# A diffusion layer's SwiGLU with seven products a tile: its sums of weights by accumulating DMA in place of VectorE

## What is computed

```
def swiglu(h, wg, wu, wd):
    return (jax.nn.silu(h @ wg) * (h @ wu)) @ wd
...
        xs = xs + gt2 * swiglu(modulate(rmsnorm(xs, g_ffn[l]), sh2, sc2), w_gate[l], w_up[l], w_down[l])
```

## Time and profile before

| | us |
|---|---|
| median of 3 runs | 937.9 (936.69 to 941.97) |
| the profiled execution | 939.53 |
| its span (first to last instruction) | 937.7 |
| TensorE busy | 915.8 (98%) |
| VectorE busy | 637.4 (68%) |
| ScalarE busy | 408.1 (44%) |
| GpSimd busy | 2.8 |
| tiles of seven products | 544.96 to 606.56, 662.88 to 761.44, 817.76 to 891.68 |

### The profile page before, as it was taken

One profiled execution on the slowest core, in us unless ns is written; L12 is line 12 of the kernel. 1 busy time (PEld: TensorE's weight loads), 2 busy tenths in 40 slices (PEclk: granted clock), 3 DMA queues, 4 the chain that ended last, 5 costly groups with the idle time before them and its releaser, 6 DMA issues.

```text
span 937.7 us, 15919 instructions
## 1 busy us (share of the span) xinstructions
PE 915.8 (98%) x6385; PEld 859.1 (92%) x6385; DVE 637.4 (68%) x1153; ACT 408.1 (44%) x809; POOL 2.8 (0%) x8
## 2 busy tenths in 40 slices
PE   5999999999999999999999999999999999999998
PEld 4689888778888899999999999999999999999998
DVE  3557898899688752332447989744699954499852
ACT  4663344666777622222246745321344421244430
POOL 0000000000000000000000000000000000000000
PEclk8899999999999999999999999999999999999999
DMA  9844343542445122422202122330222243022331
GB/s 369 325 180 159 139 151 113 162 137 68 136 147 161 54 68 91 180 68 90 68 23 90 46 91 79 102 112 24 82 79 80 78 134 90 24 72 86 116 108 71
DMA packets 33082, 104.44 MB, mean 111 GB/s; under 512 B 3696, under 2 KB 8944, under 8 KB 31856
## 3 DMA queue, kind: packets, MB, share of 16 engines
q1 hardware_dynamic: 32288, 102.64, 33.0%
q10 hardware_dynamic: 720, 0.77, 0.2%
HBM read 99.07 MB, written 4.33 MB: 110 GB/s over the span
## 4 chain that ended last, share of the span: by engine, by line
PE 91%; DVE 4%; DMA 2%; ACT 2%; SPq 1%; issue 1%; ACTq 0%; DVEq 0%
PE ps L1595 38%; PE ps L1952 25%; PE ps L1691 13%; PE ps L1899 4%; PE ps L1817 3%; PE ps L1791 2%; PE ps L1802 2%; PE ps L1644 1%; DMA x<-x_t 1%; PE ps L1715 1%; DMA x<-w_ada 1%; SPq L550 1%; DVE scr L1080 1%; ACT b L626 1%; DVE scr L1231 0%
## 5 line engine op out<-in xcount | busy, mean ns | idle before, releaser
L1043 DVE TENSOR_TENSOR w_lo<-stage,w_hi 128x1024 fp32r<-128x1024 f32 x56 | 68.4, 1222 | 76.5 <-ACT w_hi L613 76.3
L958 ACT ACTIVATE w_hi<-stage 128x512 fp32r<-128x512 f32 x114 | 71.1, 628 | 96.2 <-PE ps L1595 40.7
L1595 PE MATMUL ps<-y_hi,w_hi 128*128 128x320 f32 x480 | 109.4, 309 | 0.0
L1595 PE MATMUL ps<-y_lo,w_hi 128*128 128x320 f32 x480 | 109.3, 309 | 0.0
L1595 PE MATMUL ps<-y_hi,w_lo 128*128 128x320 f32 x480 | 109.3, 309 | 0.0
L613 ACT ACTIVATE w_hi<-stage 128x1024 fp32r<-128x1024 f32 x56 | 59.1, 1061 | 91.7 <-PE ps L1595 50.9
L1952 PE MATMUL ps<-m_hi,w_hi 128*128 128x320 f32 x304 | 93.9, 309 | 0.0
L1952 PE MATMUL ps<-m_lo,w_hi 128*128 128x320 f32 x304 | 93.9, 309 | 0.0
L1952 PE MATMUL ps<-m_hi,w_lo 128*128 128x320 f32 x304 | 93.9, 309 | 0.0
L1595 PEld LDWEIGHTS ps<-y_lo,w_hi 128*128 128x128 f32 x480 | 80.3, 188 | 0.0
L1595 PEld LDWEIGHTS ps<-y_hi,w_hi 128*128 128x128 f32 x480 | 80.2, 188 | 0.0
(11 more groups left out here) (207 smaller groups left out, 1947.6 us busy)
## 6 DMA issues: line engine op xcount, KB each, us to landing
stage<-w_main SPq DMA_DIRECT2D x118, 512.0 KB, 3.6
x<-w_ada SPq DMA_DIRECT2D x23, 512.0 KB, 4.5
qk<-w_ada SPq DMA_DIRECT2D x7, 1024.0 KB, 12.4
bb<-rpb SPq DMA_DIRECT2D x16, 256.0 KB, 4.1
qk<-w_ada SPq DMA_DIRECT2D x5, 512.0 KB, 3.8
x<-x_t SPq DMA_DIRECT2D x1, 2560.0 KB, 10.7
y_t<-x SPq DMA_DIRECT2D x8, 320.0 KB, 2.2
vf<-w_ada SPq DMA_DIRECT2D x4, 512.0 KB, 3.6
```

What stands on the lines that cost most here:

```text
L958: act.activation(w_hi[:, slot, at:at + 512], left_stage(op, g), ACT.Copy).then_inc(left_hi[op], 1)
L1043: dve.tensor_tensor(w_lo[:, slot, :], stage[:, slot, :], w_hi[:, slot, :].bitcast(F32), ALU.subtract).then_inc(lo_done, 1)
L1595: ins = pe.matmul(out[:, half, :], wt[:, w_slot, w], rt[:, rk, half * TH:(half + 1) * TH], start=start and n == 0, stop=stop and n == 2)
```

## The change

GpSimd issues the sums as DMAs that add to their destination (`accum_op=ALU.add`), five transfers of 128 x 512 (256 KB) a tile: S1 adds A22, read again from the weights in DRAM, to A21 in the stage; S3's buffer is loaded with A11 from DRAM, and A21 from DRAM is added; S2 adds S1 to A11, S4 adds S2 to A12, both from SBUF to SBUF. As there is only addition, the signs are turned: the factors are now S2 = A11 + S1, S3 = A11 + A21 and S4 = A12 + S2, and the sums of products subtract the products of S2, S3 and S4. Where one VectorE instruction made two sums at once with one operation, two instructions stand for C11/U2 and for C21/C12. The waits on the sums count by 16, the semaphore steps of a DMA. S2 is split ahead of S1 in the inner loop.

```diff
@@ block.gpsimd
+            def accumulate(op, u, at, done):
+                pool.dma_start(op, w_main[u, :, at:at + 512], accum_op=ALU.add).then_inc(done, 16)
+            for g in range(sum(FF_PARTS) - N_STD):
+                u = gate_unit(N_STD + g)
+                pool.wait_ge(*unit_arrived(u + 1))
+                accumulate(left_stage("S1", g), u + 1, 512, s1_sum)
+                if g:
+                    pool.wait_ge(left_lo["S3"], g)
+                pool.dma_start(s3_sb, w_main[u, :, 0:512]).then_inc(s3_in, 16)
+                pool.wait_ge(s1_sum, 16 * (g + 1))
+                pool.wait_ge(left_lo["A11"], g + 1)
+                pool.dma_start(left_stage("S2", g), left_stage("S1", g), accum_op=ALU.add).then_inc(s2_sum, 16)
+                pool.wait_ge(s3_in, 16 * (g + 1))
+                accumulate(s3_sb, u + 1, 0, s3_sum)
+                pool.wait_ge(s2_sum, 16 * (g + 1))
+                pool.wait_ge(left_lo["A12"], g + 1)
+                pool.dma_start(left_stage("S4", g), left_stage("S2", g), accum_op=ALU.add).then_inc(s4_sum, 16)
@@ block.scalar, left_high
-                    act.wait_ge({"S1": s1_sum, "S2": s2_sum, "S3": s3_sum, "S4": s4_sum}[op], g + 1)
+                    act.wait_ge({"S1": s1_sum, "S2": s2_sum, "S3": s3_sum, "S4": s4_sum}[op], 16 * (g + 1))
...
-                        for op in ("S1", "S2", "S3", "S4"):
+                        for op in ("S2", "S1", "S3", "S4"):
                             left_high(op, g + 1)
@@ block.vector
-            def s3(g):
...
-                dve.tensor_tensor(s3_sb, left_stage("A11", g), left_stage("S1", g), ALU.subtract).then_inc(s3_sum, 1)
-            def s1(g):
...
-                dve.tensor_tensor(left_stage("S1", g), left_stage("S1", g), left_stage("A22", g), ALU.add).then_inc(s1_sum, 1)
-            def s2(g):
...
-                dve.tensor_tensor(left_stage("S2", g), left_stage("S1", g), left_stage("A11", g), ALU.subtract).then_inc(s2_sum, 1)
-            def s4(g):
...
-                dve.tensor_tensor(left_stage("S4", g), left_stage("A12", g), left_stage("S2", g), ALU.subtract).then_inc(s4_sum, 1)
...
-                dve.tensor_tensor(two(H_C11, H_U2), of_product("A12", "S2"),
-                                  by_half[:, H_P1:H_P1 + 1, :].to_broadcast([P, 2, TH]), ALU.add).then_inc(c11_done, 1)
+                dve.tensor_tensor(by_half[:, H_C11, :], of_product("A12"), by_half[:, H_P1, :], ALU.add)
+                dve.tensor_tensor(by_half[:, H_U2, :], of_product("S2"), by_half[:, H_P1, :], ALU.subtract).then_inc(c11_done, 1)
...
-                dve.tensor_tensor(two(H_C21, H_C12), of_product("A22", "S4"), two(H_U3, H_V), ALU.add).then_inc(c12_done, 1)
+                dve.tensor_tensor(by_half[:, H_C21, :], of_product("A22"), by_half[:, H_U3, :], ALU.add)
+                dve.tensor_tensor(by_half[:, H_C12, :], of_product("S4"), by_half[:, H_V, :], ALU.subtract).then_inc(c12_done, 1)
```

More of the change, by code:

```diff
@@ L329, in hybrid_dit_program @@
         s1_sum, s2_sum, s3_sum, s4_sum = (sem(f"s{i}_sum") for i in (1, 2, 3, 4))
+        s3_in = sem("s3_in")
         t_sum, t_hi_done, t_ready = sem("t_sum"), sem("t_hi_done"), sem("t_ready")
@@ L1436, in left_low, with of_product @@
                                   ALU.subtract).then_inc(left_lo[op], 1)
-            def s3(g):
[L1439 to L1442, removed]
-                dve.tensor_tensor(s3_sb, left_stage("A11", g), left_stage("S1", g), ALU.subtract).then_inc(s3_sum, 1)
-            def s1(g):
-                dve.wait_ge(s3_sum, g + 1)
-                dve.tensor_tensor(left_stage("S1", g), left_stage("S1", g), left_stage("A22", g), ALU.add).then_inc(s1_sum, 1)
-            def s2(g):
-                dve.wait_ge(s1_sum, g + 1)
-                dve.tensor_tensor(left_stage("S2", g), left_stage("S1", g), left_stage("A11", g), ALU.subtract).then_inc(s2_sum, 1)
-            def s4(g):
-                dve.wait_ge(s2_sum, g + 1)
-                dve.tensor_tensor(left_stage("S4", g), left_stage("A12", g), left_stage("S2", g), ALU.subtract).then_inc(s4_sum, 1)
-            def of_product(op, op2=None):
-                a, b = BANK_OF[op], BANK_OF[op2 or op]
-                return ps[:, a:b + 1, 0:TH] if op2 else ps[:, a:a + 1, 0:TH].to_broadcast([P, 2, TH])
+            def of_product(op):
+                return ps[:, BANK_OF[op], 0:TH]
             def c11_u2(g):
@@ L1472, in v_sum @@
                 dve.wait_ge(c11_done, g + 1)
-                dve.tensor_tensor(by_half[:, H_V, :], ps[:, BANK_OF["S1"], 0:TH], by_half[:, H_U2, :], ALU.add).then_inc(v_done, 1)
+                dve.tensor_tensor(by_half[:, H_V, :], of_product("S1"), by_half[:, H_U2, :], ALU.add).then_inc(v_done, 1)
             def c22_u3(g):
@@ L1477, in c22_u3 @@
                 dve.wait_ge(v_done, g + 1)
-                dve.tensor_tensor(two(H_C22, H_U3), of_product("S3"), two(H_V, H_U2), ALU.add).then_inc(c22_done, 1)
+                dve.tensor_tensor(two(H_C22, H_U3), two(H_V, H_U2),
+                                  ps[:, BANK_OF["S3"]:BANK_OF["S3"] + 1, 0:TH].to_broadcast([P, 2, TH]),
+                                  ALU.subtract).then_inc(c22_done, 1)
             def c21_c12(g):
@@ L1512, in _ @@
             left_low("A11", 0)
-            s3(0)
             left_low("A12", 0)
-            s1(0)
             gated_up(1)
-            s2(0)
-            s4(0)
             t_low(2)
@@ L1539, in _ @@
                         left_low("A11", g + 1)
-                        s3(g + 1)
                     else:
@@ L1547, in _ @@
                         left_low("A12", g + 1)
-                        s1(g + 1)
                     v_sum(g)
[L1550 to L1553, removed]
+                    if not more:
                         down_low(part, 1)
@@ L1574, in _ @@
                             left_low("A11", g)
-                            s3(g)
                             left_low("A12", g)
-                            s1(g)
-                            s2(g)
-                            s4(g)
                         elif n == 5:
```

## The result

The changed kernel takes 943.49 us in the median of 13 runs (937.9 to 944.83), the kernel before 937.9 us in as many: a ratio of 1.0046 with a 95% interval of 1.0027 to 1.0065. It is slower, by 4.3 us; the forecast had 17.7 us of waiting and a time of 957 us, 19 above the median before. In a second set beside the experiments it took 943.16 us against 938.05, ratio 1.0048 (1.0029 to 1.0068).

A forecast was written before the change was run, and what follows sets the result against it. TensorE was taken to bound the kernel; late sums would make it wait 2.3, 10.4 and 5.0 us in the parts of 5, 8 and 6, together 17.7, so 939.5 + 17.7 = 957 us, range 935 to 1010.

The forecast's parts named there:

- The bound and the cover: FFN tiles: TensorE sets the time without waiting for VectorE, so removing 52 us of VectorE's sums gains 0 us.
- The figure of 49 us: VectorE: its busy time was to be 49 us less in the profile after the change.
- Splitting the instructions: VectorE, twice a tile: two instructions of 320 results for one of 640, 3 us over 19 tiles, hidden under TensorE.
- The loop: S2's sum, S4's sum, then A11's low half releasing the next S2: one turn takes 2L + 5.0 us against TensorE's 12.32.
- D: How far into a part's second tile S4's sum is there: 2L - 8.6, put at 1.4 us.
- L: Time from issue of one accumulating transfer in the row to its semaphore: 5.0 us, from 3.6 plus 1.1 plus 0.3.
- G: Lateness the sums gain with each tile once L is above 3.66 us: 2L - 7.3, put at 2.7 us.
- in time: Rival: L at most about 4.4 us, so lateness hardly reaches TensorE; no change, time 938 to 943; chance 0.32.
- The limit: TensorE first stalls for the next S2's low half, when D is above 9.5 - L, put at 4.5 us.
- Disturbed weight loads: Down units' stretches: the new transfers disturbing the weight loads was booked at nothing.
- The sign: Whole kernel: slower by more than about 0.5% 0.65, same 0.32, faster 0.03.

The follow-up runs named there:

- e4_after: The changed kernel run again unaltered, for a second trace on the same chip as the other runs; 943.16 us, ratio 1.0048.
- e5_long: The changed kernel with one more wait: S4's transfer is issued only when S3's has landed too; 982.39 us, ratio 1.0475.
- e12_quiet: The changed kernel with weight loads of the scheme's third and later tiles cut to 32 of 1024 columns; 942.4 us, ratio 1.0037.
- e8_s4late: The changed kernel with only the order changed: S4's halves are made behind A11's of the tile after; 963.23 us, ratio 1.0259.
- e6_short: The changed kernel with S4's sum on VectorE again and the other three sums by transfer; 938.21 us, ratio 1.0005.
- e2_idle: The kernel before, with five GpSimd transfers a tile beside it into a spare buffer nobody reads; 939.34 us, ratio 1.0003.

## Why the prediction was wrong

**The bound and the cover: right.** TensorE does not wait behind VectorE in the tiles, and 44 us less of VectorE's work (639.9 with the signs alone, 596.2 changed) bought nothing. The figure of 49 us was too high, since it took a sum at its full 0.69 us while the busy time counts the overlap with the next one once: 0.58 us each. Splitting the instructions cost nothing, as booked.

**The loop: right, to a tenth.** From S4's sum to A11's low half it was forecast 5.0 us and measured 5.06; D, how far into the second tile S4's sum lands, was 2L - 8.6 = -0.6 at the measured L, and S4 landed at 676.45, 0.55 us before that tile's start at 677.00.

**L: the step that failed.** The time of one link, a transfer in the row, was put at 5.0 us; the turn of 13.10 us gives (13.10 - 5.06) / 2 = 4.0. The parts: 0.57 us from release to issue, 3.3 us from issue to landing (0.86 of them GpSimd's instruction), 0.35 to 0.43 until the next transfer's issue, and an occasional 0.3 to 2 us more. By the prediction's own wording, from issue to semaphore, L was even less, 3.3 us in the median, and the 0.57 and 0.35 had no term. I had built the 5.0 from loads out of DRAM. The transfers that read DRAM again do take 4.6 and 5.0 us, but the two in a row go from SBUF to SBUF. Whether the read of the destination costs anything, for which I had doubled the bytes, is not shown: no plain transfer from SBUF to SBUF was run. By the fit of the Trainium skill ("DMA: Bandwidth & Descriptors", Anatomy of one DMA, SWDGE path) the estimate is 2.6 us for 256 KB, 0.7 under the measured landing of 3.3; mine was 1.7 over it. With G = 2L - 7.3, the lateness gained in a tile, an error of 1 us in L is 2 us a tile: 0.8 us and not 2.7. By the prediction's own sum L = 4.0 gives no loss at all, its rival "in time".

**The limit: the second error, the other way.** I took the next S2's low half as what is wanted first, D up to 9.5 - L, here 5.5 us. Inside the tiles that is borne out by e4_after (waits at D = 5.6). In a part's last tile something is wanted sooner: the second down unit's low half is 9.8 us behind S4's sum and wanted at 12.32, so D may be 2.5 us. Lateness of the eighth tile: -0.55 + 6 x 0.78 = 4.1; 4.1 - 2.5 = 1.6 us, the wait of the trace. For the parts of 6 and 5 the same sum gives D = 2.6 and 1.8, no wait of weight, as measured. With this limit and L = 5.0 the forecast would have been 32 us; e5_long, with a turn of 15.4, lost 37 in the tiles.

**What was not in it.** In e4_after the wait of 3 us is followed by some 3.5 us at the lower clock, which cost 1.8 us more. The two traces of the changed kernel lost 2.0 and 6.2 us in the FFN, on both sides of the 4.3 us that the ratio says: 1.6 and 4.4 us by lateness, for S4's transfer took over 5 us twice in the second, and 0.4 and 1.8 in the down units.

**Disturbed weight loads: right at nothing.** They land after 3.7 us in the median, 3.6 before. The reverse case, transfers stretched by loads, plays little part in the changed kernel (e12_quiet); with another order of work it does, and e8_s4late shows the price.

**The sign.** The chance of 0.65 stood on slower by over 0.5%; the ratio is just inside that bound, with an interval that reaches to both sides of it. That the kernel came out slower at all, as forecast, is luck: at the measured L the path of the prediction gives nothing, and the loss came through the limit that it had overlooked.

## What to carry to other kernels

Taking work off an engine that nobody waits for gains nothing, and handing it to DMA puts a latency where there was 0.7 us of work: count how many such transfers stand in a row in one turn, add what the in-order engines do between them, and compare with the pace of the engine that sets the time. One accumulate in a row was free here (e6_short), two were 0.8 us a tile over. When lateness builds up, look for the earliest deadline in the last round of a loop, where other work takes the place of the usual, and look at what a reordering does to the moment at which loads are released.

## What the runs showed of the hardware

- In the changed kernel an accumulating transfer of 256 KB by GpSimd lands 3.3 us after its issue from SBUF to SBUF and 5.0 us from DRAM (medians); a plain one from DRAM after 3.8 us.
- GpSimd's own instruction takes 0.86 us for an accumulating transfer and 0.57 us for a plain one, and 0.86 with VectorE 73% (the changed kernel) or 90% busy (e2_idle). Issued some 0.55 us behind another it is recorded with 1.15 to 1.24 us, which includes the 0.3 us that the first still takes.
- The same SBUF-to-SBUF transfer takes 7.3 to 7.7 us, once 8.6, when loads of 512 KB are issued in the same microsecond (e8_s4late), and 6.1 us in the median where the transfer ahead of it is in flight (e2_idle).
- In the FFN of all these traces TensorE stood still eight times for 2.6 to 3.8 us, and each time the granted clock was at 0.50 to 0.57 in a stretch of 2 us within the next 4. Behind thirty waits of 0.75 to 1.73 us it was 1.00 for those 4 us.
